# A transformer layer with 16,384 small experts: marks, dots and row fetches of the expert part set to other units, and each expert low half made in two pieces on GpSimd

## What is computed

```
def peer_ffn(x, wq, subkeys, u, v):
    q = (xt @ wq) ...                                   # 8 heads, two halves of 64
    sub = jnp.einsum('thpd,hpkd->thpk', q, subkeys)     # 128 keys per half
    s_top, i_top = lax.top_k(sub, 16)
    cand = s_top[:, :, 0, :, None] + s_top[:, :, 1, None, :]
    sc, ci = lax.top_k(cand.reshape(..., 256), 16)
    eid = (i1 * 128 + i2).reshape(t_len, 128)           # 128 experts per token
    gate = jax.nn.softmax(sc, axis=-1).reshape(t_len, 128)
    h = gelu(einsum('cd,ced->ce', xc, u[ec]))
    return einsum('ce,ced->cd', gate * h, v[ec])
```

## Time and profile before

| | |
|---|---|
| median of 3 runs | 1681.92 us (1679.8 to 1683.86) |
| profiled execution, its own time | 1681.57 us |
| its span, first to last instruction | 1679.8 us, mean granted clock 0.995 |
| PE busy | 1641.3 us, 98% of the span |
| DVE, POOL, ACT busy | 1221.6, 838.9 and 692.0 us |
| expert units | from about 529 to 1148 us of the span |

### The profile page before, as it was taken

The page is one execution under the profiler, slowest core; times in us unless marked ns, Lnnn a source line. Parts: engine busy times, 40 slices in busy tenths (PEclk is TensorE's granted clock), DMA queues, the critical chain, the costliest instruction groups (busy, mean ns, idle before and its releaser), DMA issues.

```text
span 1679.8 us, 24143 instructions
## 1 busy us (share of the span) xinstructions
PE 1641.3 (98%) x9013; PEld 1439.6 (86%) x9013; DVE 1221.6 (73%) x2375; ACT 692.0 (41%) x1030; POOL 838.9 (50%) x492
## 2 busy tenths in 40 slices
PE   9999999999999999899999999979999999999997
PEld 7778777788889999899999998978888888888886
DVE  3586895512173976799799977845988888888886
ACT  4545545522333443344544544423333333333342
POOL 6332232444551667687787798874432234333312
PEclk9999999999999999999999999999999999999999
DMA  5121121243331568798988899999999999999952
GB/s 206 64 76 51 57 82 63 88 150 98 128 113 38 174 211 261 252 338 302 346 318 318 320 350 387 373 392 361 406 388 350 370 386 350 378 385 346 376 203 88
DMA packets 126499, 417.61 MB, mean 249 GB/s; under 512 B 12976, under 2 KB 32432, under 8 KB 124848
## 3 DMA queue, kind: packets, MB, share of 16 engines
q1 hardware_dynamic: 70320, 232.81, 39.6%
q0 software_dynamic: 36864, 134.23, 21.4%
q10 hardware_dynamic: 19200, 49.03, 7.5%
HBM read 364.91 MB, written 50.86 MB: 248 GB/s over the span
## 4 chain that ended last, share of the span: by engine, by line
PE 83%; DVE 6%; DMA 6%; POOL 2%; ACT 1%; issue 1%; SPq 0%; ACTq 0%; DVEq 0%
PE ps L1422 16%; PE ps L1423 15%; PE ps L1424 15%; PE ps L1682 10%; PE ps L1681 10%; PE ps L1684 10%; DMA u_got<-u_rows,eid 3%; PE ps L1793 2%; DVE u_got L1146 1%; DMA raw<-u_units 1%; PE ps L1534 1%; POOL w_lo L525 1%; DVE hits L1289 1%; PE ps L1486 1%; DVE right L1296 1%
## 5 line engine op out<-in xcount | busy, mean ns | idle before, releaser
L1422 PE MATMUL ps<-tok_hi,w_hi 128*128 128x384 f32 (+1 forms) x1472 | 527.5, 358 | 12.4 <-POOL w_lo L525 5.6
L1424 PE MATMUL ps<-tok_hi,w_lo 128*128 128x384 f32 (+1 forms) x1472 | 518.2, 352 | 0.0
L1423 PE MATMUL ps<-tok_lo,w_hi 128*128 128x384 f32 (+1 forms) x1472 | 518.2, 352 | 0.0
L584 ACT ACTIVATE w_hi<-raw 128x1024 fp32r<-128x1024 f32 x330 | 349.3, 1059 | 409.8 <-PE ps L1684 295.1
L525 POOL TENSOR_TENSOR w_lo<-raw,w_hi 128x1024 fp32r<-128x1024 f32 x128 | 311.0, 2431 | 127.8 <-ACT w_hi L584 77.2
L481 POOL TENSOR_TENSOR w_lo<-raw,w_hi 128x1024 fp32r<-128x1024 f32 x76 | 181.9, 2398 | 315.7 <-ACT w_hi L584 315.5
L1422 PEld LDWEIGHTS ps<-tok_hi,w_hi 128*128 128x128 f32 x1472 | 277.4, 188 | 44.0 <-issue 17.0
L542 POOL DMA_INDIRECT v_got<-v_rows,eid x128 | 158.7, 1240 | 295.3 <-DVE own L1158 277.2
L1681 PE MATMUL ps<-w_hi,gh_hi 128*128 128x512 f32 x760 | 295.7, 389 | 0.0
L1682 PE MATMUL ps<-w_lo,gh_hi 128*128 128x512 f32 x760 | 295.7, 389 | 0.0
L1424 PEld LDWEIGHTS ps<-tok_hi,w_lo 128*128 128x128 f32 x1472 | 277.3, 188 | 18.1
(11 more groups left out here) (248 smaller groups left out, 1775.9 us busy)
## 6 DMA issues: line engine op xcount, KB each, us to landing
raw<-u_units SPq DMA_DIRECT2D x128, 512.0 KB, 4.7
raw<-v_rows SPq DMA_DIRECT2D x128, 512.0 KB, 6.7
raw<-w_units SPq DMA_DIRECT2D x78, 512.0 KB, 3.4
gate_d<-stage ACTq DMA_DIRECT2D x12, 2048.0 KB, 11.4
gelu_d<-gelu_t ACTq DMA_DIRECT2D x120, 192.0 KB, 4.9
gelu_in<-gelu_d SPq DMA_DIRECT2D x30, 768.0 KB, 7.8
gate_in<-gate_d SPq DMA_DIRECT2D x28, 768.0 KB, 12.6
gate_in<-gate_d SPq DMA_DIRECT2D x2, 1536.0 KB, 16.0
```

Of the source, the lines that this page charges most:

```text
L584: act.activation(hi_of(n), raw[:, n % RAW, :], ACT.Copy).then_inc(hi_done, 1)
L1422: pe.matmul(out_, l_hi, r_hi, start=start, stop=False)
L1423: pe.matmul(out_, l_hi, r_lo, start=False, stop=False)
L1424: return pe.matmul(out_, l_lo, r_hi, start=False, stop=stop)
```

## The change

It alters constants, three conditions and one helper. The second, third and fourth blocks are marked from units 31, 62 and 93 on (33, 64 and 95 before). DVE is to have done 14, 49, 84 and 114 dots by units 31, 62, 93 and 115 (11, 41, 71 and 106). Sixteen rows, not ten, count as early, and turn 31 of POOL is the first that may fetch beyond them. The first exponential stands behind ACT's unit 9 (12 before), the others behind units 26, 52 and 83 (30, 58 and 89). `expert_lo` subtracts 512 columns, then calls `fetch`, which fetches the turn's last row, then subtracts the other 512; the other rows of a turn are fetched ahead of its wait for `right_set`, as before. Ahead of the rows of `v`, POOL waits until all dots are done.

```diff
--- before.py
+++ after.py
@@ -70,10 +70,10 @@
 GATE_SCALE = 2.0 ** 15
 FIRST_UNITS = 16
 STEPS = 22
-MARK_AT = {1: 33, 2: 64, 3: 95, 4: 115}
+MARK_AT = {1: 31, 2: 62, 3: 93, 4: 115}
 TAIL = MARK_AT[4]
-DOT_PACE = ((FIRST_UNITS + 5, 0), (MARK_AT[1], 11), (MARK_AT[2], 41), (MARK_AT[3], 71), (TAIL, 106), (P - 3, P))
-EARLY, EARLY_SLOTS = 10, 3
+DOT_PACE = ((FIRST_UNITS + 5, 0), (MARK_AT[1], 14), (MARK_AT[2], 49), (MARK_AT[3], 84), (TAIL, 114), (P - 3, P))
+EARLY, EARLY_SLOTS = 16, 3
 U_SLOTS, V_SLOTS = 5, 6
 FMA_START, FMA_END = 2, P - 12
 KEPT = 8
@@ -518,12 +518,17 @@
                     pool.memset(sk_raw[:], 0.0).then_inc(sk_zero, 1)
                 split_lo(n)
 
-            def expert_lo(k):
+            def expert_lo(k, fetch=lambda: None):
 
                 n = U_EXP + k + LO_AHEAD
                 pool.wait_ge(hi_done, n + 1)
-                pool.tensor_tensor(w_lo[:, n % RAW, :], raw[:, n % RAW, :], w_hi[:, n % RAW, :].bitcast(F32),
-                                   ALU.subtract).then_inc(lo_pool, 1)
+                for a in range(2):
+                    cols = slice(a * DM // 2, (a + 1) * DM // 2)
+                    ins = pool.tensor_tensor(w_lo[:, n % RAW, cols], raw[:, n % RAW, cols],
+                                             w_hi[:, n % RAW, cols].bitcast(F32), ALU.subtract)
+                    if a == 0:
+                        fetch()
+                ins.then_inc(lo_pool, 1)
 
             def get_u(e):
 
@@ -555,11 +560,13 @@
             pool.wait_ge(eid_set, 1)
             rows_to(EARLY_SLOTS)
             for k in range(FIRST_UNITS, P):
-                rows_to(min(EARLY, dots_by(k - 1) + EARLY_SLOTS) if k < MARK_AT[1] + 1 else dots_by(k - 1) + U_SLOTS)
+                rows = min(EARLY, dots_by(k - 1) + EARLY_SLOTS) if k < MARK_AT[1] else dots_by(k - 1) + U_SLOTS
+                rows_to(rows - 1)
                 if groups_in(k):
                     pool.wait_ge(right_set, groups_in(k).stop)
-                expert_lo(k)
+                expert_lo(k, lambda: rows_to(rows))
             rows_to(P)
+            pool.wait_ge(dot_done, P)
             for s in range(2):
                 pool.wait_ge(stage_out[s], 16 * (NB // 2))
             for e in range(P):
@@ -804,7 +811,7 @@
 
             for k in range(FIRST_UNITS):
                 expert_unit(k)
-                if k == FIRST_UNITS - 4:
+                if k == FIRST_UNITS - 7:
                     gate_exp(0)
             def take_group(m):
                 take_gates(2 * m)
@@ -814,7 +821,7 @@
                 for m in groups_in(j - 1):
                     take_group(m)
                 expert_unit(j)
-                if j + 6 in (MARK_AT[1] + 3, MARK_AT[2], MARK_AT[3]):
+                if j + 10 in (MARK_AT[1] + 5, MARK_AT[2], MARK_AT[3]):
                     gate_exp(marking_at(j) + 1)
 
             def finish_norm(t):
```

## The result

The changed kernel takes 1684.97 us (median of 19 runs, 1683.81 to 1687.51), the kernel before 1680.43 (19 runs, 1674.81 to 1684.07). The ratio is 1.0029, with a 95% interval of 1.0022 to 1.0037: slower, where 0.4% faster was forecast. The profiled execution has a span of 1683.8 us. Here are its stretches, cut where those of the earlier trace rows are cut by PE's work: from 669.40 to the start of unit 37, on to the third mark stage, on to unit 115, and the last units.

A forecast was written before the change was run, and what follows sets the result against it. PE was taken as full from 703.90 to 975.20, with 24.4 us recoverable at front, back and tail. 1681.57 + 9.0 (front) - 3.3 (back) - 11.5 (tail) = 1675.8 us, 0.4% faster; range 1667 to 1685.5.

The forecast's parts named there:

- the two pieces: POOL's low halves: two pieces take 2.6 us, 0.2 more for each of 128 halves, covered by PE, so no cost.
- the middle: Second and third mark stages: ten more dots, 12 us, fit into DVE's 22.8 us of idle time, so nothing lost.
- the back: Last third of the marks: fewer dots per unit give back 3.3 of 3.8 us; bounds 3.8 and a loss of 6.
- the tail: Last units: fewer rows remain, the gate load lands in about 14 us, 11.5 us gained; bounds 13.2 and 3.
- the front: First marks: unit 33 starts at 693.3, 8.1 us lost plus 0.9 for the clock, 9.0 in all; bounds 3.9 and 12.
- POOL holds pace: Last units: nine rows instead of 17 remain behind turn 115, so POOL needs 2.6 + 1.2 fetches against PE's 4.16.
- The slot of row 16: First mark: row 16 takes row 15's slot, so POOL's turn 31 waits for dot 15, behind the mark, delaying unit 33.
- row 3's fetch: Front: POOL fetches row 3 in turn of unit 22 whatever DVE does, so dot 3 starts 1.1 us earlier, not 10.35.
- The first rival: The tail stays, the gate load being slow by itself: 3 us of gain there, 1684.3 us in all; chance 0.13.
- The third: POOL becomes the bound at the back, its pieces waiting for marks: 7 us lost there, 1686.1 us; chance 0.10.
- The second: The front costs nothing more, unit 33 waiting no longer than unit 34 did: 1667.8 us; chance 0.10.
- the fourth: Front and tail cancel: a front loss of 11 to 12, a tail gain of 8 to 9: 1681 us; chance 0.12.

The follow-up runs named there:

- experiment 1: The changed kernel with each low half made in one piece of 1,024 columns again, all row fetches of a turn ahead of it: 1677.05 us, ratio 0.998.
- experiment 5: The changed kernel with the two pieces kept, but all row fetches of a turn ahead of its wait and pieces: 1684.45 us, ratio 1.0022.
- experiment 3: The changed kernel with the first gate load placed behind the raw tile of unit 127, not that of unit 123: 1676.88 us, ratio 0.998.
- 11: The changed kernel with two pieces and all row fetches early, run once more for a second trace: 1681.21 us in its one run.
- experiment 12: The changed kernel with one piece and two fills of an unused tile in each turn of POOL: 1687.77 us, ratio 1.0045.
- experiment 9: The changed kernel with one piece and one fill of an unused 128x128 tile on POOL in each turn: 1678.68 us, ratio 0.9997.
- experiment 2: The changed kernel with 15 early rows in place of 16, so row 16 goes into the buffer of row 13: 1680.4 us, ratio 1.0001.
- experiment 10: The changed kernel with one piece, 15 early rows, late gate load, and the pace of the dots started at unit 18, not 21: 1658.76 us, ratio 0.9875.
- experiment 6: The changed kernel with one piece, but the turn's last row still fetched behind the turn's waits, just ahead of the low half: 1691.1 us, ratio 1.0067.

## Why the prediction was wrong

**The step that failed** is *the two pieces*: "While PE takes 4.16 or more per unit and POOL 2.6 and one fetch of 0.95, PE covers it", so a price of nothing. Taking the pieces out (experiment 1) gives 8 us back by the medians, and the pieces by themselves (experiment 5) cost 7.4. The size of a piece was nearly right (a low half costs 0.30 us more than before, 0.2 was forecast and 0.26 was the bound, 33.3 us in all), and PE does wait for low halves at few places. But a comparison of POOL's time with PE's in each unit leaves out what POOL's lead does. It decides when rows are fetched and raw tiles reloaded. In the kernel before, the lead is 7.2, 7.3 and 5.3 us over units 36 to 61, 62 to 92 and 93 to 114, and falls to 1.2 only in the tail; in the changed kernel it is 3.3 us and less from the first of these on. Three terms moved at once, as the comparison with experiment 1 shows: the middle from 0 to +3.9, the back from -4.5 to -2.5, and the tail from -11.3 to -4.8: 12.4 us, of which the front gave 2.3 back (by the medians the pieces cost 8).

In the tail the way from the lead to the loss is seen in the traces: the low half of unit 119 comes late, raw tile 123 is loaded late, SP's queue is fuller when the gate load is issued, the load lands later, and raw tile 124 behind it. With the load moved (experiment 3) the tail gains 8.4 us with the pieces still in. The forecast's "POOL holds pace" was true there (a lead of 1.6 us ahead of the tail and 1.75 in it), but an engine that holds pace does not win back a lead that it has lost earlier. In the middle and at the back the lead is argued, not shown. DVE waits longer for rows at the back (24.4 us for 6.6), but the middle's loss does not follow the lead: +2.0 at leads of 4.3 and 4.1 us (experiment 5), +3.8 at 5.1 and 4.7 (11), +3.9 at 3.3 and 2.7 (changed kernel), +13.1 at 3.9 and 4.9 (12). How the price of the pieces divides between their own time and their meetings with DVE is not settled: experiment 9 had half of the dose (4 us of 8) and, by the medians, a fifth of the effect (1.6 us of 7.4), and in experiment 12 the marks were longer too.

**The other terms, once the pieces are out.** In the profiled executions the schedule alone (experiment 1) gains 6.1 us where 5.8 was forecast, stage by stage within 1.3 us; by the medians beside each other it gains 2.6 (1677.05 for 1679.63), so part of that agreement is the luck of two traces. The slot of row 16 (confirmed by experiment 2), row 3's fetch that keeps the exponential from paying (17.59 us of wait, and experiment 10, which moves that fetch), the free dots of the middle and POOL's rest in the tail were read rightly. Two slips in the sums change nothing: two units of 4.16 less 0.3 are 8.0, not 8.1, and the 9.8 and 2.29 us of the tail make 12.1, for which 11.5 was put without a stated reason.

**The tail** came out right in experiment 1 for a reason that was only half right. The load was priced by the rows issued beside it, at 1.4 us each. In the changed kernel four were issued while it ran, as forecast, and it took 20.0 us, not 14.0 (eight were landing or issued, for fourteen before). The runs show a share, not a price per row: SP's queue had 41.4% of the engines before, 47.4% now and 45.6% with one piece. It moved 3.45 MB during the load before, 3.68 now and 2.45 with one piece: what shortened the load there was a queue with less in it. The first rival, "the tail stays" (1684.3), has this time within 0.7 us, by luck: it has the tail at -3, for -4.8, and nothing for the middle's +3.9, and with the front at +9.0 for +7.5 the errors nearly cancel.

**The rivals.** The third, with POOL as the bound, came nearest to the mechanism, POOL made slow by its pieces, and has 1686.1 us, but it put the loss into the last third of the marks; there PE idles 1.10 us only. The second fell with POOL's wait of 8.70 us, and the fourth with a tail of -4.8.

**Left open:** why the front alone is 2.3 us worse with one piece than with two, and why it varies from +3.8 to +9.9 among kernels whose front differs by a fill or a fetch's place; a trace or two for each doesn't tell.

## What to carry to other kernels

An engine that is not the bottleneck may still run its lead down, and holding pace later does not bring it back: before splitting its instruction, look at how far it is ahead of its consumer, and what else (fetches, buffers set free, loads behind them) follows its clock. Where a load stands in a queue ahead of tiles that are needed sooner, and the DMA engines are full, its place can be worth more than its length: one number changed gave 0.5% in the changed kernel (0.15% in the kernel before, where POOL was the next limit). And where an idle engine is given an earlier start, find the next thing that it waits for, and move that too: with row 3's fetch moved, the front went from a loss to a gain.

## What the hardware did that was not expected

A second piece of a GpSimd subtraction costs 0.30 us here, and a DVE instruction can stand until a GpSimd one has ended: `right` took 3.24 us in place of 1.22 beside a low half of 2.60, and `hits` 2.294 on average in experiment 6. The Trainium skill (SBUF — State Buffer, "Who interferes with whom") has this as an exclusive lock on ports that the two engines share, for DVE instructions with two inputs in SBUF; the rows agree. Half-long pieces did not shorten the marks reliably: a pair took 3.11 us in the changed kernel and 3.28 and 3.39 in experiments 5 and 11, for 3.20 with one piece.

The DMA engines were shared between the two queues at 41 to 47% for SP's while row fetches were in flight, and it had 88% without them: 1536 KB took 9.1 us without row fetches beside them and 20.0 with them and a fuller queue, while all queues together moved 339 and 404 GB/s.
